# Two attention maps of a unit in separate PSUM banks, compressed products last, and the memory units' turn ahead of the values

## What is computed

```
first block, token_mixer, 4 heads with two maps each, 2 query tiles of 128:
    sc = q . k * scale - slope * dist, causal;  p = softmax(sc)       (two maps: m = 0, 1)
    out = (p[map 0] - lam * p[map 1]) @ v
second block, hybrid_mixer, 8 NSA heads (2 key groups), 4 MLA, 4 FOX heads:
    NSA: out = g0 * softmax(q.kc)@vc + g1 * softmax(q.k_slc)@v_slc + g2 * softmax(q.k_win)@v_win
    MLA: softmax(q.k * 96**-0.5)@v     FOX: softmax(q.k + decay)@v
second block, memory_cross_attention, 4 heads over 256 memory rows: softmax(q.k / 8)@v
```

## Time and profile before

| | |
|---|---|
| median of three runs | 3072.76 us (3070.82 to 3072.85) |
| the profiled execution's own time | 3084.24 us |
| its span | 3082.5 us |
| PE busy | 2997.6 us, 97% |
| DVE, ACT busy | 1898.7 us (62%), 1347.3 us (44%) |
| mean granted TensorE clock | 0.988 of full |
| first block's units | 52 to 90 us, 1043 to 1081 us |
| mix units | 2102 to 2240 us, and again from 2641 us |
| memory units | 2321 to 2334 us, and in the second layer |

### The profile page before, as it was taken

The page is one execution under the profiler, slowest core; times in us unless marked ns, Lnnn a source line. Parts: engine busy times, 40 slices in busy tenths (PEclk is TensorE's granted clock), DMA queues, the critical chain, the costliest instruction groups (busy, mean ns, idle before and its releaser), DMA issues. The chain is left out here.

```text
span 3082.5 us, 53809 instructions
## 1 busy us (share of the span) xinstructions
PE 2997.6 (97%) x20906; PEld 2616.4 (85%) x20906; DVE 1898.7 (62%) x3659; ACT 1347.3 (44%) x2053; POOL 132.0 (4%) x62
## 2 busy tenths in 40 slices
PE   8999999999999999999999999999998999999898
PEld 7699889898897869889989899797777979777797
DVE  4489854787547648975578755745535464553546
ACT  4443444444444544244445444444425444442544
POOL 0061000000000007000000000000000000000000
PEclk9999999999999999999999999999999999999999
DMA  5244355544545424345554455451234555123454
GB/s 214 91 171 150 137 191 180 195 144 163 191 180 188 164 106 169 136 151 191 181 187 147 167 191 197 178 212 69 96 137 159 183 184 212 69 96 137 159 182 150
DMA packets 68022, 493.59 MB, mean 160 GB/s; under 512 B 7576, under 2 KB 7584, under 8 KB 8352
## 3 DMA queue, kind: packets, MB, share of 16 engines
q1 hardware_dynamic: 67568, 490.42, 44.1%
q0 software_dynamic: 304, 1.06, 0.1%
HBM read 490.39 MB, written 1.06 MB: 159 GB/s over the span
## 5 line engine op out<-in xcount | busy, mean ns | idle before, releaser
L781 DVE TENSOR_TENSOR ring_l<-ring,tile_h 128x1024 fp32r<-128x1024 f32 x648 | 764.8, 1221 | 668.0 <-ACT tile_h L736 663.8
L736 ACT ACTIVATE tile_h<-ring 128x1024 fp32r<-128x1024 f32 x644 | 645.8, 1052 | 532.9 <-PE ps L667 445.4
L635 PE MATMUL ps<-x_h,tile_h 128*128 128x256 f32 x2016 | 575.5, 285 | 2.2 <-issue 2.2
L636 PE MATMUL ps<-x_l,tile_h 128*128 128x256 f32 x2016 | 570.0, 283 | 0.0
L637 PE MATMUL ps<-x_h,ring_l 128*128 128x256 f32 x2016 | 569.9, 283 | 0.0
L635 PEld LDWEIGHTS ps<-x_h,tile_h 128*128 128x128 f32 x2016 | 386.4, 192 | 3.1 <-issue 2.9
L636 PEld LDWEIGHTS ps<-x_l,tile_h 128*128 128x128 f32 x2016 | 386.5, 192 | 0.2
L637 PEld LDWEIGHTS ps<-x_h,ring_l 128*128 128x128 f32 x2016 | 386.3, 192 | 0.0
L740 ACT ACTIVATE arena<-ps 128x512 f32 (+1 forms) x160 | 95.8, 599 | 433.7 <-PE ps L637 346.7
L665 PE MATMUL ps<-tile_h,w_even 128*128 128x512 f32 x640 | 249.5, 390 | 3.6 <-DVE w_even L806 3.6
L665 PE MATMUL ps<-tile_h,w_odd 128*128 128x512 f32 x640 | 249.3, 390 | 0.7 <-DVE w_odd L806 0.7
(11 more groups left out here) (330 smaller groups left out, 5602.0 us busy)
## 6 DMA issues: line engine op xcount, KB each, us to landing
ring<-stream SPq DMA_DIRECT2D x464, 1024.0 KB, 4.8
cs<-consts SPq DMA_DIRECT2D x1, 1712.5 KB, 8.4
x<-x_in SPq DMA_DIRECT2D x1, 1024.0 KB, 4.9
arena<-scratch POOLq DMA_DIRECT2D x1, 1024.0 KB, 7.8
out<-x SPq DMA_DIRECT2D x2, 512.0 KB, 2.7
tab<-table SPq DMA_DIRECT2D x1, 1.0 KB, 8.2
scratch<-arena POOLq DMA_DIRECT2D x1, 12.0 KB, 5.0
```

The lines of the kernel that those rows point to most:

```text
L635: nc.tensor.matmul(out, uh[:, c, f], x_h[:, c, :], start=(c == 0), stop=False)
L636: nc.tensor.matmul(out, uh[:, c, f], x_l[:, c, :], start=False, stop=False)
L736: nc.scalar.activation(tile_h[:, j % 2, n], slot(k + j)[:, n], ACT.Copy).then_inc(hi_ready, 1)
L781: nc.vector.tensor_tensor(low_of(k + j)[:, n], slot(k + j)[:, n], tile_h[:, j % 2, n].bitcast(F32), ALU.subtract).then_inc(lo_ready, 1)
```

## The change

1. **Scores.** Map 0 of an even unit goes to bank 4 and map 1 to bank 5; of an odd unit to banks 2 and 3. PE's wait for its own map 0 is gone.
2. **Memory scores** (`all_scores`) keep their banks. They are written as one map of each unit (map 0 of units 0 and 2, map 1 of units 1 and 3), and then the other one. PE waits twice for `sc_first`, ahead of the second map of units 0 and 2.
3. **Values.** The products of both maps come first, then the compressed products of both.
4. **Memory units, turn.** They turn into banks 6 and 7 by turns, and turn(u+1) stands ahead of values(u).
5. **First block's fills** use banks 7, 1, 7, 0. The third waits for the release of bank 7 by the first, the last for the copy of bank 0. ACT copies bank 0 between the exps of unit 6 and the copy of turn(5), and bank 1 behind the last unit.
6. **Second block's heads.** Banks 0 and 1 by turns take one pair each. `heads_out` copies one pair (128x256) at units 5, 9, 13, 17, 19, 21, 23 and behind the last, and PE waits for that copy before a bank is opened again (`opened`). `oT` moves to where the small weights `smB` lay, since it is now written while the fills use `tile_h`.

The semaphore `ob_ev` counts 8 a layer in place of 4. The arithmetic is the same.

```diff
+        def raw_scores(u, m, klen, banks):
+            if banks is None:
+                return ps[4 + m if u % 2 == 0 else 2 + m][:, 0:klen]
+            return ps[banks[u]][:, m * 256:m * 256 + klen]
+
+        def turned_bank(u, banks):
+            return ps[6 if banks is None else 6 + u % 2]
...
             def score(u):
-                if u >= 2 and banks is None:
+                if u >= 2:
                     pe.wait_ge(sm_max, base + (u - 1))
-                bank = ps[4 + u % 2 if banks is None else banks[u]]
                 for m in range(2):
-                    klen = units[u]["keys"]
-                    last = scores(units[u], m, bank[:, m * 256:m * 256 + klen])
-                    if m == 0:
-                        last.then_inc(sc_first, 1)
-                        pe.wait_ge(sc_first, base + (u + 1))
+                    last = scores(units[u], m, raw_scores(u, m, units[u]["keys"], None))
                 last.then_inc(sc_mm, 1)
+
+            def all_scores():
+                for turn in range(2):
+                    for u in range(len(units)):
+                        if turn and u % 2 == 0:
+                            pe.wait_ge(sc_first, (base - done_b) // UNITS_B * 2 + (u // 2 + 1))
+                        m = (u + turn) % 2
+                        last = scores(units[u], m, raw_scores(u, m, units[u]["keys"], banks))
+                        if turn:
+                            last.then_inc(sc_mm, 1)
+                        elif u % 2:
+                            last.then_inc(sc_first, 1)
 
             def turn(u):
                 pe.wait_ge(sm_p, base + (u + 1))
-                if u >= 1:
+                if banks is None and u >= 1:
                     pe.wait_ge(pt_ev, base + u)
+                if banks is not None and u >= 2:
+                    pe.wait_ge(pt_ev, base + (u - 1))
                 for m in range(units[u]["turned"]):
                     for kt in range(units[u]["keys"] // P):
-                        last = nc.tensor.transpose(ps[6][:, (2 * m + kt) * P:(2 * m + kt + 1) * P],
+                        last = nc.tensor.transpose(turned_bank(u, banks)[:, (2 * m + kt) * P:(2 * m + kt + 1) * P],
                                                    E[:, u % 2, m, kt * P:(kt + 1) * P], ident)
                 last.then_inc(pt_mm, 1)
 
-            for u in range(2 if banks is None else len(units)):
-                score(u)
+            if banks is None:
+                score(0)
+                score(1)
+            else:
+                all_scores()
             if lead is not None:
                 lead()
+            if banks is not None:
+                turn(0)
             for u in range(len(units)):
-                turn(u)
+                if banks is None:
+                    turn(u)
+                elif u + 1 < len(units):
+                    turn(u + 1)
                 if u + 2 < len(units) and banks is None:
                     score(u + 2)
                 if fill is not None:
                     fill(u, 0)
                 pe.wait_ge(pt_ev, base + (u + 1))
-                for m in range(2):
-                    last = values(units[u], m, PT[:, u % 2, m, :, :])
-                last.then_inc(pv_mm, 1)
+                if opened is not None:
+                    opened(u)
+                values(units[u], PT[:, u % 2, :, :, :]).then_inc(pv_mm, 1)
...
+        def diff_values(w, pt):
+
             n = w["keys"] // P
             for kt in range(n):
-                diff_values.last = nc.tensor.matmul(ps[w["qt"]][:, w["h"] * P:(w["h"] + 1) * P], pt[:, kt, :],
-                                                    vt[:, kt, w["h"] * P:(w["h"] + 1) * P],
-                                                    start=(kt == 0), stop=(kt == n - 1))
-            return diff_values.last
+                last = nc.tensor.matmul(ps[w["qt"]][:, w["h"] * P:(w["h"] + 1) * P], pt[:, 0, kt, :],
+                                        vt[:, kt, w["h"] * P:(w["h"] + 1) * P], start=(kt == 0), stop=(kt == n - 1))
+            return last
...
+        FILL_BANK = (7, 1, 7, 0)
...
-                    if m == 0 and n >= 3:
-                        pe.wait_ge(proj_ev, l * 12 + 6 + (n - 2))
+                    if m == 0 and n == 2:
+                        pe.wait_ge(proj_ev, l * 12 + 7)
+                    if m == 0 and n == 3:
+                        pe.wait_ge(o_copied, l * TT + 1)
...
+                if u == 5:
+                    heads_kept(0)
+
+            def heads_kept(tt):
+                act.wait_ge(pv_mm, l * UNITS_A + 4 * (tt + 1))
+                nc.scalar.activation(O[:, tt, :], ps[tt][:, :], ACT.Copy).then_inc(o_copied, 1)
...
-        oT = room(8 * SEQ, GATES + BLK * 512).rearrange("p (b n) -> p b n", b=8)
-        sq = room(TT * 512).rearrange("p (t n) -> p t n", t=TT)
+        oT = smB.rearrange("p (b n) -> p b n", b=8)
+        sq = room(TT * 512, GATES + BLK * 512 + 8 * SEQ).rearrange("p (t n) -> p t n", t=TT)
...
+        HEADS_FROM = [0, 4, 8, 12, 16, 18, 20, 22]
+        HEADS_END = HEADS_FROM[1:] + [24]
...
+            def out(m):
+                return ps[pair % 2][64 * m:64 * m + 64, qt * P:(qt + 1) * P]
+
+            def v(m, kt):
+                h = 2 * pair + m
+                if kind in (1, 2):
+                    return vsw[:, kt, (kind - 1) * P + (pair // 2) * HD:][:, 0:HD]
+                return mv2[:, kt, h, :] if kind == "mla" else (fv if kind == "fox" else xv)[:, kt, h * HD:(h + 1) * HD]
+
+            for m in range(2):
+                for kt in range(n):
+                    last = nc.tensor.matmul(out(m), v(m, kt), pt[:, m, kt, :], start=(kt == 0 and kind != 2),
+                                            stop=(kt == n - 1 and kind != 1), skip_group_check=(kind in (1, 2)))
             if kind == 2:
                 g = pair // 2
-                last = nc.tensor.matmul(out, vc[0:CN[qt], g * HD:(g + 1) * HD], PcT[0:CN[qt], qt, h, :],
-                                        start=False, stop=True, skip_group_check=True)
+                for m in range(2):
+                    last = nc.tensor.matmul(out(m), vc[0:CN[qt], g * HD:(g + 1) * HD], PcT[0:CN[qt], qt, 2 * pair + m, :],
+                                            start=False, stop=True, skip_group_check=True)
...
+            def opened(u):
+                if u in HEADS_FROM[2:]:
+                    pe.wait_ge(ob_ev, l * 8 + (HEADS_FROM.index(u) - 1))
+
+            pe_units(pe, done_b + l * UNITS_B, mix_units, b_scores, b_values, gate_piece, lambda: gate_run(0, 16),
+                     opened=opened)
...
-            def heads_out(b):
-                act.wait_ge(pv_mm, done_b + l * UNITS_B + (20, 20, 22, 24)[b])
-                nc.scalar.activation(oT[:, 2 * b:2 * b + 2, :], ps[b][:, :].rearrange("p (a n) -> p a n", a=2),
+            def heads_out(g):
+                act.wait_ge(pv_mm, done_b + l * UNITS_B + HEADS_END[g])
+                nc.scalar.activation(oT[:, 2 * g if g < 4 else 2 * g - 7, :], ps[g % 2][:, 0:SEQ],
                                      ACT.Copy).then_inc(ob_ev, 1)
 
             def between_units(u):
                 if u <= 20 and u % 2 == 0:
                     gate_out(u // 2)
-                if u >= 21:
-                    heads_out(u - 21)
+                if u - 1 in HEADS_END:
+                    heads_out(HEADS_END.index(u - 1))
```

More of the change, by code:

```diff
@@ L402, in program, with pe_units @@
         pt_mm, pt_ev, pv_mm = sem("pt_mm"), sem("pt_ev"), sem("pv_mm")
-        def pe_units(pe, base, units, scores, values, fill=None, lead=None, banks=None):
+        def raw_scores(u, m, klen, banks):
[4 more added lines that the diff above has]
+            return ps[6 if banks is None else 6 + u % 2]
+        def pe_units(pe, base, units, scores, values, fill=None, lead=None, banks=None, opened=None):
@@ L451, in exps @@
                 for m in range(2):
-                    raw = S[:, u % 2, m, 0:klen] if banks is None else ps[banks[u]][:, m * 256:m * 256 + klen]
+                    raw = S[:, u % 2, m, 0:klen] if banks is None else raw_scores(u, m, klen, banks)
                     last = nc.scalar.activation(E[:, u % 2, m, 0:klen], raw, ACT.Exp,
@@ L467, in act_units @@
                 nc.scalar.activation(PT[:, u % 2, 0:maps, 0:n, :],
-                                     ps[6][:, :].rearrange("p (m k q) -> p m k q", m=2, k=2)[:, 0:maps, 0:n, :],
+                                     turned_bank(u, banks)[:, :].rearrange("p (m k q) -> p m k q", m=2, k=2)
+                                     [:, 0:maps, 0:n, :],
                                      ACT.Copy).then_inc(pt_ev, 1)
@@ L479, in bias @@
                     dve.wait_ge(sm_exp, base + (u - 1))
-                raw = ps[4 + u % 2 if banks is None else banks[u]][:, :]\
-                    .rearrange("p (m k) -> p m k", m=2)[:, :, 0:klen]
                 if banks is not None:
+                    raw = ps[banks[u]][:, :].rearrange("p (m k) -> p m k", m=2)[:, :, 0:klen]
```

(31 more changed lines are left out.)

16 lines of the change are left out of this document (6 added, 10 removed).

## The result

| | before | changed |
|---|---|---|
| first comparison, median | 3072.81 us (3070.82 to 3073.68, 4 runs) | 3031.47 us (3024.01 to 3036.06, 4 runs) |
| repeated, median | 3074.88 us (3061.12 to 3089.49, 23 runs) | 3026.77 us (3023.72 to 3037.83, 6 runs) |
| profiled execution, its span | 3084.24 us, 3082.5 us | 3028.12 us, 3026.3 us |
| mean granted clock in it | 0.988 | 0.990 |

The ratio of the first comparison is 0.9846, 95% interval 0.9822 to 0.9869, that of the repetition 0.9841 (0.9816 to 0.9866). All ten runs of the changed kernel together have a median of 3028.1 us; 3028.0 was forecast. That the two agree to 0.1 us is luck: the ten runs lie between 3023.7 and 3037.8 us.

What follows compares the result with a forecast made beforehand. PE, in order and busy 77.24 of 78 us in the mix stage, was taken as the bound, so its gaps are kernel time; terms summed to 44.8 us, 3072.8 less 44.8 giving 3028.0 us, range 3020 to 3040.

Steps and rivals of the forecast that it cites:

- scores of 64 rows: NSA scores behind the lead: second map overlaps the first and costs nothing, 0.75 or 0.54 us a score, 18.5 us.
- lead of block 2: Two lead scores of block 2 lose their waits between maps: 0.94 us a layer, 1.9 us.
- MLA: MLA scores contract over 96 rows, so maps can't overlap; only the wait goes, 0.22 us for 8 units, 1.8 us.
- FOX: FOX scores: maps don't meet; the wait less the change of mode goes, 8 x 0.12 = 1.0 us.
- `heads_out` at unit 22: Second block: the head copy that held up ACT's copy at unit 22 goes, 0.35 us a layer, 0.7 us.
- first block: Scores behind the lead get shorter, but DVE's low parts hold turns 1, 4 and 6: 2.9 us a layer, 5.8.
- memory units: Turn ahead of values lets last values start sooner: 1.0 us a layer, bounds 0 and 1.2, 2.0 us in all.
- Does something else come late: Mix stage: DVE's probabilities (1.16 us ahead of the turn) and ACT's copy still come in time; costed at nothing.
- The rival of DVE as the bound: Mix stage: late probabilities cost each of 16 qt-1 pairs of scores 0.5 us, 8 us lost: 3036 us; chance 0.10.
- One or two added stretches: Unit stages: one or two more half-clock stretches of PE, 1.7 us each, counted inside the forecast range.
- The rival "more comes back": Half-clock stretch at mix stage's start vanishes, 1.7 us a layer; first block's turn not held, 4.2 more: 3021 us; chance 0.08.
- maps that don't overlap across two banks: 64-row scores: only the wait goes, 6.2 us in place of 18.5, lead and first block less too: 3044.5 us; chance 0.05.

Runs made afterwards that it cites:

- wait_back: The changed kernel, but PE waits again between the two maps of a score (not in the memory units): 3067.27 us (10 runs).
- mem_order_warm: clock_gap with memory turn(u) behind values(u-1) again, plus 16 unread transposes ahead of turn(0) and 5 behind each turn: 3019.14 us (one run).
- clock_gap: The changed kernel with five unread 256-column matmuls in PE's 0.61 us wait ahead of the compression: 3016.65 us (5 runs).
- values_only: The kernel before, with only kind-2 values reordered, both 128-row products first and both compressed products behind them: 3068.54 us (10 runs).

## Why the prediction was right, point by point

Columns: forecast, and what the profiles show.

| term | forecast | measured |
|---|---|---|
| scores of 64 rows | 18.5 | 2 x (8 x 0.75 + 6 x 0.54) = 18.4 |
| lead of block 2 | 1.9 | 2 x 0.92 = 1.8 |
| MLA | 1.8 | 2 x (0.28 + 0.06 + 2 x 0.32) = 2.0 |
| FOX | 1.0 | 8 x 0.13 = 1.0 |
| values | 13.1 | 8 x 0.71 + 8 x 0.92 = 13.0 |
| `heads_out` at unit 22 | 0.7 | 2 x 0.4 = 0.8 |
| first block | 5.8 | 2 x 2.76 = 5.5 |
| memory units | 2.0 | 2.4 at full clock, 1.7 with the stretch of layer 0 |
| clock at the start of the mix stage | 0 | 2 x 1.5 = 3.0 |

- **The sum.** The measured terms sum to 47.2 us (44.8 forecast), with 1.7 for the memory units. With the 9.6 us of layer 0's long stretch that is 56.8 of the 56.1 us between the profiles; the other 0.7 is small differences elsewhere. The mechanisms and sizes were right, the last digits were not: the forecast left out 3.0 us of clock and started from a median of three runs, 3072.8, where 23 runs of before give 3074.9, and these two errors nearly cancel.
- **Scores.** Rows 4 were the right case to price by. wait_back settles it (28.9 us for 29.0). The rule of the Trainium skill, "TensorE: Matmul & The Clock Gate", section "Part 3: Packing small matmuls", weighed in the prediction, would have made the first memory unit 0.4 us a layer later. The trace doesn't agree: the eight maps start their passes in pairs 0.22 us apart, so a pair of maps takes 0.43 us, and the first probabilities are 0.12 us later than before (turn(0) at 4.26 us for 4.14), near the 0.1 forecast.
- **Does something else come late.** DVE's probabilities of unit 5 led the turn by 1.15 us (1.16 before) and ACT's copy was ready 1.76 us ahead of the values (1.8 forecast). The rival of DVE as the bound falls for the mix stage.
- **First block.** The named turns wait: 1, 4 and 6. It took 34.96 us in place of 37.72, 2.76 less; idle ahead of turn(0) was 1.23 us (forecast about 1.4).
- **Memory.** The full-clock gain is 1.2 us a layer, forecast 1.0, and mem_order_warm puts it on the turn ahead of the values. What the prediction lacked here is the clock: the stage that the change made shorter is one in which PE now idles for 2.3 us, and it runs partly at half clock in one layer or both in all six profiles with the new order whose PE isn't filled there. In clock_gap's layer 1 and wait_back's layer 0 the last values come at 11.7 us, later than the 11.3 of before. "One or two added stretches" was the right size, by luck of a bound and not by this reading.
- **The rival "more comes back"** was half right. The half-clock stretch at the start of the mix stage is gone in both layers: 20.0 us fewer a layer between first score and last values, 18.5 of them from the terms above. values_only, which has no such stretch either, needs 10.68 us from first score to first values against 12.15, which prices it at 1.5. That the change removes the stretch isn't shown: values_only keeps all waits between maps and has the stretch in neither layer, wait_back keeps them too and has it in both. What the profiles show is that none of the 18 mix stages without the waits has it. The first block's turn was held as forecast. This rival's own terms, 3028.0 - 3.4 - 4.2, give 3020.4 and not 3021, and its 4.2 isn't worked out.
- **The profiled execution.** It was to come out near 3039.4 and took 3028.1. The prediction took both kernels' profiles to be equally far above their medians; the 11.5 us of before were mostly one stretch of 20.48 us at half clock, some 10 us, which isn't in every run. A profile's own time should have been set against its stretches of half clock first.
- **MLA.** One of the two 128-key scores of a layer saved only 0.06 us; why stays open.
- Of the other rivals, maps that don't overlap across two banks were not seen, and among the unit stages the clock fell in the memory units alone: in the mix stage it was 1.00.

## What to carry to other kernels

A window that counts PE as 99% busy can hide waits between small matmuls; look at PEld's idle time and at the start-to-start time of a piece. Two products in different halves of the rows, in two banks and without a wait between them, cost as much as one here; and products of one height belong together, so that they can overlap and the height changes less often. Idle time of PE has a second price, the clock behind it: find the half-clock stretches, ask which have PE as their bound, and fill only the gaps ahead of those, with unread matmuls if nothing else is there.

## What the runs showed of the hardware that was not expected

- 0.61 us of idle time on PE was followed by 17 to 20 us at half clock (0.50, PE busy for 16.74 of 17.00 us) in eight of ten places profiled. Five matmuls in that gap (0.8 us) gave back 8 us in layer 1.
- A half-clock stretch of 3.41 us costs 1.5 us at the start of the mix stage, 0.65 in the memory units (10.76 against 10.11 us), 1.0 behind one normalization (at 1985.2) and nothing behind another (at 998.8).
- Run to run, the spread of these kernels (3061 to 3089 us before) is mostly the granted clock: span times clock of before varies less (3038 to 3046).
- FOX's two 64-row products of 256 columns cost 0.63 us together when they stand side by side, and 0.63 us each with full-height products between them; in a run of 64-row products alone such a pair costs 0.43 us.
